# Gate products of a gated linear recurrence: 128x128 blocks with zeros against 64x64 quarters

## The reference, cut to what matters

```python
xb = xc.reshape(B, S, LRU_BLOCKS, LRU_BW)            # S = 256, 8 blocks of 64
r = jax.nn.sigmoid((jnp.einsum('bsni,nij->bsnj', xb, wa).reshape(B, S, LRU_W) + ba))
i = jax.nn.sigmoid((jnp.einsum('bsni,nij->bsnj', xb, wi).reshape(B, S, LRU_W) + bi))
log_a = -LRU_C * r * jax.nn.softplus(-lam)
a = jnp.exp(log_a)
bterm = jnp.sqrt(-jnp.expm1(2.0 * log_a)) * i * xc
_, h = lax.associative_scan(_lin_combine, (a, bterm), reverse=reverse, axis=1)
```

## Time and profile before

| | |
|---|---|
| median of 3 runs | 1420.13 us (1419.36 to 1421.99) |
| span of the profiled execution, first to last instruction | 1415.0 us |
| outside the span, against the median | 5.13 us |
| PE busy | 1204.4 us (85%) |
| PE weight loads | 617.2 us (44%) |
| DVE busy | 614.2 us (43%) |
| ACT busy | 204.7 us (14%) |
| POOL busy | 50.0 us (4%) |
| HBM read | 464.71 MB, 329 GB/s over the span |

### The profile page before, as it was taken

How to read it: one execution, slowest core, us unless ns; L and a number is a source line. 1 busy time by engine, 2 the same in 40 slices (tenths; PEclk the granted TensorE clock), 3 DMA queues, 4 the chain that set the end, 5 groups by cost and what they waited for, 6 DMA issues and landing times.

```text
span 1415.0 us, 27580 instructions
## 1 busy us (share of the span) xinstructions
PE 1204.4 (85%) x10094; PEld 617.2 (44%) x10095; DVE 614.2 (43%) x1368; ACT 204.7 (14%) x464; POOL 50.0 (4%) x85
## 2 busy tenths in 40 slices
PE   7999999999999996486879988877998878776675
PEld 6757577665674442132334433333443333222232
DVE  1525434344587753333435434343544434333343
ACT  1212022120253310010101101011110110100101
POOL 0000000001011000000000000000000000000000
PEclk9999999999999999889999999999999999998898
DMA  9912173121731799999999999999899999999997
GB/s 358 334 60 91 60 282 134 60 90 60 262 148 48 311 413 427 428 428 428 428 428 428 428 429 427 428 428 385 371 429 428 427 429 429 429 428 427 429 429 296
DMA packets 62562, 466.30 MB, mean 330 GB/s; under 512 B 6592, under 2 KB 10428, under 8 KB 37948
## 3 DMA queue, kind: packets, MB, share of 16 engines
q1 hardware_dynamic: 59196, 462.07, 79.0%
q0 software_dynamic: 624, 2.10, 0.5%
q10 hardware_dynamic: 2704, 1.60, 0.4%
HBM read 464.71 MB, written 1.05 MB: 329 GB/s over the span
## 4 chain that ended last, share of the span: by engine, by line
PE 60%; DMA 33%; issue 3%; DVE 2%; ACT 1%; ACTq 1%; SPq 0%; POOLq 0%; POOL 0%; DVEq 0%
DMA ring<-in_w_up_dram 25%; PE bank L1366 18%; PE bank L926 12%; PE bank L933 9%; PE bank L1378 6%; DMA ring<-in_w_down_dram 6%; PE bank L1116 3%; PE bank L1395 2%; PE bank L1347 2%; DMA x_mem<-in_w_down_dram 2%; PE bank L1313 1%; PE bank L1173 1%; ACTq L877 1%; ACT mem L886 1%; PE bank L1224 0%
## 5 line engine op out<-in xcount | busy, mean ns | idle before, releaser
L1366 PE MATMUL bank<-ring,mem 128*32 128x512 f32 x2832 | 393.5, 655 | 132.9 <-DMA ring<-in_w_up_dram 109.3
L1366 PEld LDWEIGHTS bank<-ring,mem 128*32 128x32 f32 x2832 | 113.8, 119 | 320.2 <-issue 302.0
L926 PE MATMUL bank<-ring 128*128 128x256 f32 x768 | 168.7, 380 | 0.0
L1378 PE MATMUL bank<-ring,mem 128*32 128x256 f32 x2624 | 159.0, 382 | 10.6 <-DMA ring<-in_w_down_dram 10.3
L926 PEld LDWEIGHTS bank<-ring 128*128 128x128 f32 x768 | 145.1, 190 | 21.1 <-issue 1.7
L884 ACT ACTIVATE const<-bank 64x512 f32<-64x512 f32 x48 | 28.6, 595 | 816.6 <-PE bank L1366 816.6
L2321 DVE TENSOR_TENSOR mem<-bank,const 64x512 f32<-64x512 f32 x48 | 32.8, 683 | 232.3 <-PE bank L1366 232.3
L933 PE MATMUL bank<-ring 128*128 128x512 f32 (+2 forms) x320 | 123.8, 542 | 1.3 <-DVE ring L1654 1.3
L1378 PEld LDWEIGHTS bank<-ring,mem 128*32 128x32 f32 x2624 | 77.0, 109 | 81.2 <-issue 26.5
L2315 DVE TENSOR_TENSOR mem<-bank,const 128x256 f32<-128x256 f32 x48 | 20.5, 428 | 153.7 <-PE bank L1347 151.9
L933 PEld LDWEIGHTS bank<-ring 128*128 128x128 f32 x320 | 60.6, 193 | 56.3 <-issue 50.7
(11 more groups left out here) (395 smaller groups left out, 1121.9 us busy)
## 6 DMA issues: line engine op xcount, KB each, us to landing
ring<-in_w_up_dram SPq DMA_DIRECT2D x64, 2048.0 KB, 29.7
ring<-in_w_gate_dram SPq DMA_DIRECT2D x53, 2048.0 KB, 32.1
ring<-in_w_down_dram SPq DMA_DIRECT2D x53, 2048.0 KB, 28.3
ring<-in_w_in_dram SPq DMA_DIRECT2D x19, 2048.0 KB, 11.9
x_mem<-in_w_gate_dram SPq DMA_DIRECT2D x11, 2048.0 KB, 32.1
x_mem<-in_w_down_dram SPq DMA_DIRECT2D x10, 2048.0 KB, 27.0
ring<-in_w_out_dram SPq DMA_DIRECT2D x6, 2048.0 KB, 8.2
ring<-in_w_in_dram SPq DMA_DIRECT2D x2, 1056.0 KB, 6.9
```

What stands on the lines that cost most here:

```text
L926: i = mm(b[:, S * j:S * j + S], w[:, k, P * (c + j):P * (c + j + 1)], hT[:, k, :], start=(k == 0), stop=(k == KC - 1))
L1366: i = mm(gate_up_bank(q), xT[:, at:at + T], w[q // 2][:, c, 512 * (q % 2):512 * (q % 2 + 1)], start=(h == 0 and c == 0), stop=(h == 1 and ...
L1378: i = mm(YB[quarter[q], 0:QD], hT_sb[:, at:at + T], w[:, c, cols_of[q]], start=(h == 0 and c == 0), stop=(h == 1 and c == 3), skip_group_c ...
```

## The change

The zero halves go. `lru_w` becomes 64 columns per matrix instead of 128, with the block of even number on partitions 0-63 and the odd one on 64-127. Each 128x128 product becomes two 64x64 ones. PE's array is addressed in quarters: a product's rows are where its input lies, its columns where its output goes. For the even chunk of a pair the two products stay on their own partitions ("straight"); for the odd chunk they go to the other half ("crossed"), so that the four products of a pair of chunks use four different quarters. A unit now holds one chunk for both gates: unit 6 + 4d + 2h is chunk 2h (straight), unit 7 + 4d + 2h is chunk 2h + 1 (crossed). ACT reads a straight chunk as before, and a crossed one in two halves of 64 partitions, from the other half, so that the result lands where it belongs. The wait for both banks of a pair now stands ahead of its products. The zeroing and its semaphore are gone.

```diff
-        lru_w = mem5[:, 0:2048].rearrange("p (u n) -> p u n", u=16)
+        lru_w = mem5[:, 0:1024].rearrange("p (u n) -> p u n", u=16)
...
-            pool.wait_ge(sc_ready, DEPTH * SC_L)
-            pool.memset(lru_w[:, :, :], 0.0).then_inc(lru_w_zero, 1)
...
-            act.wait_ge(lru_w_zero, 1)
+            act.wait_ge(sc_ready, DEPTH * SC_L)
...
-                        act.dma_start(lru_w[HD * j:HD * (j + 1), 8 * d + 4 * g:8 * d + 4 * g + 4, HD * j:HD * (j + 1)],
+                        act.dma_start(lru_w[HD * j:HD * (j + 1), 8 * d + 4 * g:8 * d + 4 * g + 4, :],
...
+            low, high = slice(0, HD), slice(HD, P)
             for d in range(2):
-                for g in range(2):
-                    for h in range(2):
-                        b = unit2(6 + 4 * d + 2 * g + h)
-                        for j in range(2):
-                            c = 2 * h + j
-                            i = A(gate[d][g][:, c, :], b[:, S * j:S * (j + 1)], ACT.Tanh, scale=0.5,
-                                  bias=half_b[:, 8 * g + 4 * d + c:8 * g + 4 * d + c + 1])
+                for h in range(2):
+                    for crossed in range(2):
+                        b, c = unit2(6 + 4 * d + 2 * h + crossed), 2 * h + crossed
+                        for g in range(2):
+                            at = 8 * g + 4 * d + c
+                            for to_rows, from_rows in (((low, high), (high, low)) if crossed else ((slice(0, P), slice(0, P)),)):
+                                i = A(gate[d][g][to_rows, c, :], b[from_rows, S * g:S * (g + 1)], ACT.Tanh, scale=0.5,
+                                      bias=half_b[to_rows, at:at + 1])
                         used2(i)
...
-            for u in range(8):
-                b = pj2(6 + u)
-                for j in range(2):
-                    i = mm(b[:, S * j:S * (j + 1)], lru_w[:, 2 * u + j, :], xc[:, 2 * (u % 2) + j, :], start=True,
-                           stop=True, skip_group_check=True)
-                i.then_inc(pj_ready, 1)
+            low, high = slice(0, HD), slice(HD, P)
+            for d in range(2):
+                for h in range(2):
+                    even, odd = 2 * h, 2 * h + 1
+                    straight, crossed = pj2(6 + 4 * d + 2 * h), pj2(7 + 4 * d + 2 * h)
+                    for g in range(2):
+                        cols = slice(S * g, S * (g + 1))
+                        for b, c, from_rows, to_rows in ((straight, even, low, low), (straight, even, high, high),
+                                                         (crossed, odd, low, high), (crossed, odd, high, low)):
+                            i = mm(b[to_rows, cols], lru_w[from_rows, 8 * d + 4 * g + c, :], xc[from_rows, c, :], start=True,
+                                   stop=True, skip_group_check=True)
+                            if g and to_rows == (high if c == even else low):
+                                i.then_inc(pj_ready, 1)
```

More of the change, by code:

```diff
@@ L374, in build @@
         dve_step = sem("dve_step")
-        xc_ready, lru_w_in, lru_w_zero = sem("xc_ready"), sem("lru_w_in"), sem("lru_w_zero")
+        xc_ready, lru_w_in = sem("xc_ready"), sem("lru_w_in")
         qk_ready, lru_ready, y2_ready = sem("qk_ready"), sem("lru_ready"), sem("y2_ready")
```

## The result

Before the change 1420.43 us (median of 12 runs), after it 1424.74 us (12 runs). The ratio is 1.0028, with a 95% interval of 1.0019 to 1.0037: 2.7 to 5.3 us slower. The prediction said 1420.9, with a range up to 1423.2.

What follows compares the result with a forecast made beforehand. The prediction took loads started after the third mixing block as the bound, with ACT's tanh there holding PE: span 1415.0 + 0.79 us later start of group 3 + 5.13 outside it = 1420.9 us, range 1418.8 to 1423.2.

Steps and rivals of the forecast that it cites:

- What bounds the kernel: Second part: loads at a fixed rate, started after the third mixing block, whose path moves the end one for one.
- The products: Gate products on PE: four quarters side by side, 3.45 us instead of 6.91, plus 0.20 per block PE waited for.
- Rival (a): Gate products: quarters of different rows sharing a bank run two at a time, total 1421.8 us; chance 0.08.
- Rival (b): Gate products: quarters run one at a time, +6.9 us, total 1427.0; chance 0.05.
- The tanh: ACT reading the gate products: 24 tanh instead of 16 at 0.36 us each, 2.9 us more for ACT.
- The clock: PE in the third mixing block: granted clock stays at 1.00 from 396 to 420 us, costing nothing.
- rival (c): PE's clock falls after idling, 1.4 us more once, total 1422.3; chance 0.10, of which 0.04 with more than one fall.
- The sum: Whole kernel: span 1415.0 + 0.79 for the later group 3, plus 5.13 outside the span, 1420.9 us; chance 0.70.
- What was queued behind: After the gate products: PE's 0.79 us goes through; ACT's exponential, 1.3 us late, and DVE's work stay hidden.
- Zeroing and loads: Before the products: dropping POOL's 1.80 us of zeroing at 344 us, with the same eight DMAs, changes 0 us.
- (d): ACT's tanh: half the partitions cost less, group 3 could start 0.7 us early, total 1419.5; chance 0.04.
- (e): Banks between PE and ACT do not hold PE; the products' 3.46 us come through whole, total 1416.7; chance 0.03.

Runs made afterwards that it cites:

- e2_whole: Changed kernel with crossed units read whole, 16 tanh instead of 24, halves not changing places; keys turned 13.23 us after the first product.
- e7_uncrossed: Changed kernel with each half of a crossed unit read to its own partitions, still 24 tanh; keys turned 17.16 us after the first product.
- e3_filler: Changed kernel plus 18 unused PE instructions ahead of its two long waits; keys turned 15.77 us after the first product.
- e1_pairs: Changed kernel with a crossed unit's tanh reordered, both gates of one half, then of the other; keys turned 16.88 us after the first product.
- e6_anti: Changed kernel with 128x128 products and zero blocks again, keeping its units and 24 tanh; keys turned 16.55 us after the first product.
- e5_banks_pairs: Changed kernel with four more banks for blocks 3 and 4 and tanh reordered by halves; 1415.36 and 1416.28 us, ratios 0.9962 and 0.9971 to before.

## Why the prediction was wrong

**What bounds the kernel**: right. In the 14 profiles with unchanged routing it is 935.7 to 939.0 us from SP's issue to the end of the span (951 to 952 in e2_whole and e7_uncrossed, which route otherwise), without a trend by kernel, and what the mixing block lost or won arrived at SP's issue. Those 3 us of scatter are as large as what is looked for, which is why the table stops there.

**The products**: right. A block in four quarters takes 1.02 us to the next line (403.78 to 404.80 in e3_filler), where 0.86 + 0.20 was written, and 64 in a row take 3.62. Rival (a) fell: the straight products write one bank from different rows, and so do the crossed ones, and 16 instructions still took 1.09 us, where two at a time would have taken 1.9. The rule of the Trainium skill (page "TensorEngine Tiling (Array Packing)", section "Gotcha 1: PSUM Pressure") that different row tiles cannot access one bank simultaneously does not show as time here, with the tiles on different partitions of the bank; the measurement decides. Rival (b) fell with it.

**The tanh**: mis-sized, and the first part of the miss. Their number and their bound on PE were right; the step "half the partitions cost a full instruction: 8 x 0.36" took the pace of a run of like instructions for one that changes partitions at every step. Two blocks took 5.57 us instead of 4.47. That moved group 3 by 1.85 us (e3_filler, clock up) instead of the forecast 0.79. Rows 6 gave lengths of single instructions and could not show it; the prediction's rows held no pace of neighbours on different partitions, and its bounds left that term out.

**The clock**: this is the step that failed. The sum put the waits at their own length and the clock behind them at nothing ("The clock is 1.00 from 396 to 420"); rival (c) stood there with 0.10, the worse part of it with 0.04. The fall came in all five profiles, and cost more than the 1.4 us set on one fall: in the first one 0.89 in block 4 (9.65 against 8.76) and 2.17 in group 3 (9.18 against 7.01). Three errors: the idle time was under-priced with the tanh (2.98 and 1.71 us instead of 2.7 and 1.2); the row held against the fall, a stretch with PE busy 1.12 of 3.20 us at a clock of 1.00, was no proof, as its two pauses of 1.28 and 0.83 us stand in every kernel, and in eight of the 16 profiles the clock falls within 0.2 us of the end of the second; and the 1.4 us were read from a fall of 3.4 us, where this one lasted 6.8. In these runs the clock fell where the first wait was 2.74 to 2.99 us (the change, e1_pairs, e7_uncrossed) and stayed up where it was 1.77 or 1.42 (e2_whole, e6_anti). That is one profile each for e2_whole and e6_anti, and the place at 360 us shows what one profile is worth (stretch from 360 to 364 us, before and after):

```profile
360.00:364.00 4.00, 3.17 (x17) 2.62 (x16) 2.71 (x7) 1.12 (x4) 0.70 (x1) 1.00 1.05 399
360.00:364.00 4.00, 3.17 (x14) 2.46 (x13) 3.29 (x8) 1.45 (x4) 0.70 (x1) 0.72 1.06 403
```

PE has the same instructions and the same pauses in both kernels here, and the clock stays up in one and falls at 361.7 us in the other. So the fall comes with idle times of 1.3 and 0.8 us in some executions and not in others, and that waits of 1.4 to 1.8 us never do is not shown. The row had come from an execution without the fall, by luck.

**The sum** against the first profile: 0.79 forecast + 1.06 more for the tanh (unit 9, which block 4 waits for, is read 7.60 us after the first product instead of 6.58; the last 0.04 is PE's start after it) + 0.89 + 2.17 for the clock + 0.11 (group 3's half is 7.01 in e3_filler, 6.90 before) = 5.02 us. Measured 18.83 - 13.81 = 5.02. It had to come out, since each term is a difference of two neighbouring profiles; what carries weight is that the fall is gone in every kernel in which the waits are gone. Without the fall, e3_filler's loss of 1.96 us up to SP's issue would have been inside the stated range, although the tanh were mis-sized there too.

**What was queued behind**: right. DVE's and ACT's covers held, and nothing of the delay was absorbed. ACT's exponential of direction 0 came 13.2 us after the first product instead of the forecast 10.9, and ACT still stood 6.12 us ahead of direction 1's. **Zeroing and loads**: the loads landed in time in every kernel; what the zeroing costs by itself was not tried alone, but e6_anti, which has it back, starts its first product at 398.53, no later than the seven other profiles with falls at 64 and 360 us (398.76 to 399.04). **Rivals (d) and (e)**: e2_whole makes (d) true by an edit, 0.7 us early as worked out, and e5_banks_pairs makes (e) true: with the banks out of the way 3.2 us of the product's 3.46 come through to the turning of the keys.

What stays open: why the runs put e5_banks_pairs 3.8 to 5.0 us below the kernel before when its profiles say 3.0. The intervals reach from 2.6 to 7.4, so it may be scatter.

## What to carry over

When one engine is made twice as fast and its partner was only 15% quicker than it, the partner is the new bound: count the buffers between them first, and give them more (here four idle banks) before or together with the faster product. On a path of matmuls, work that is saved but leaves a hole is not free: price the hole with the clock at half speed for what comes behind it. And instructions that go to changing partitions on ACT want sorting, so that neighbours use the same ones.

## What the hardware showed that I had not expected

ACT starts a 256-column tanh 0.36 us after the last one if both read from the same start partition and write to the same one, and 0.48 us after it if either changes between 0 and 64, crossed or not. PE did the products with their zero blocks, in twice the time (e6_anti), or 18 filler instructions more (e3_filler), and turned the keys 2.3 and 3.1 us earlier for it, because the granted clock stayed at 1.00. And in all 16 profiles the clock falls at one or two of three places ahead of the products (64, 236 to 240 and 360 us), and with them the first gate product moves between 396.0 and 399.4 us.
